# A two-block transformer on one core: the opening reordered across three engines, and the first output product opened with two tiles

## The reference, cut to what matters

```
def diff_attn_layer(x, norm_g, w_in, w_out, ...):
    h = rms_norm(x, norm_g)
    q, k, v, gate = jnp.split(h @ w_in, 4, axis=-1)
    q = partial_rope(q.reshape(B, L, 2 * A_HEADS, A_HEAD_DIM), cos, sin)
    k = partial_rope(k.reshape(B, L, 2 * A_HEADS, A_HEAD_DIM), cos, sin)
    ...
    o = diff_attention(q, k, v, lam, cid)            # 8 heads
    o = rms_norm(o, subln_g) * (1.0 - lambda_init)
    o = o.reshape(B, L, D_MODEL) * jax.nn.silu(gate)
    return x + o @ w_out
```

## Time and profile before

| | |
|---|---|
| time, median of 3 runs | 2648.57 us (2648.28 to 2649.2) |
| time of the profiled execution | 2649.55 us |
| its span, first to last instruction | 2647.7 us |
| mean granted TensorE clock | 0.989 |
| busy: TensorE, its weight load, VectorE, ScalarE, GpSimd | 98%, 92%, 37%, 46%, 72% |
| a load of half a weight tile (512 KB), issue to landing | 3.6 us (median) |

### The profile page before, as it was taken

One profiled execution on the slowest core, in us unless ns is written; L12 is line 12 of the kernel. 1 busy time (PEld: TensorE's weight loads), 2 busy tenths in 40 slices (PEclk: granted clock), 3 DMA queues, 4 the chain that ended last, 5 costly groups with the idle time before them and its releaser, 6 DMA issues.

```text
span 2647.7 us, 54457 instructions
## 1 busy us (share of the span) xinstructions
PE 2591.1 (98%) x22558; PEld 2442.5 (92%) x22558; DVE 978.4 (37%) x1361; ACT 1225.4 (46%) x1504; POOL 1902.3 (72%) x786
## 2 busy tenths in 40 slices
PE   7999999999999999999999999999999999999998
PEld 7899999999999999999898989999998898998986
DVE  5444444316666330314354544314371120120211
ACT  4344444555666654535353444345453343443443
POOL 5666677676666787757574757688698888888886
PEclk8999999999999999989999999999999999999999
DMA  5454455454444566545353535466566566666664
GB/s 187 138 156 143 144 147 156 129 175 138 135 145 142 151 184 213 151 120 163 115 160 109 161 112 160 128 191 209 158 177 188 178 189 203 186 187 190 185 189 151
DMA packets 119614, 426.51 MB, mean 161 GB/s; under 512 B 12784, under 2 KB 17008, under 8 KB 119152
## 3 DMA queue, kind: packets, MB, share of 16 engines
q1 hardware_dynamic: 114560, 416.55, 52.8%
q10 hardware_dynamic: 4848, 6.82, 0.8%
HBM read 419.12 MB, written 4.19 MB: 160 GB/s over the span
## 4 chain that ended last, share of the span: by engine, by line
PE 92%; DVE 4%; ACT 3%; issue 1%; DMA 0%; POOL 0%; SPq 0%; DVEq 0%; ACTq 0%; POOLq 0%
PE ps L315 15%; PE ps L218 15%; PE ps L220 15%; PE ps L227 15%; PE ps L241 5%; PE ps L249 5%; PE ps L243 5%; PE ps L1893 3%; PE ps L306 3%; PE ps L302 2%; PE ps L301 2%; PE ps L1183 2%; ACT wh L199 1%; PE ps L840 1%; PE ps L1785 1%; PE ps L1787 1%
## 5 line engine op out<-in xcount | busy, mean ns | idle before, releaser
L2886 POOL TENSOR_TENSOR wl<-raw,wh 128x1024 fp32r<-128x1024 f32 x782 | 1902.1, 2454 | 728.2 <-ACT wh L199 727.1
L199 ACT ACTIVATE wh<-raw 128x2048 fp32r<-128x2048 f32 x391 | 748.2, 1914 | 647.0 <-DMA raw<-weights 173.9
L218 PE MATMUL ps<-hh,wh 128*128 128x256 f32 (+1 forms) x3056 | 752.1, 285 | 3.5 <-DVE hl L351 2.3
L220 PE MATMUL ps<-hl,wh 128*128 128x256 f32 (+1 forms) x3056 | 749.0, 284 | 0.0
L218 PEld LDWEIGHTS ps<-hh,wh 128*128 128x128 f32 x3056 | 577.3, 189 | 8.6 <-issue 4.2
L220 PEld LDWEIGHTS ps<-hl,wh 128*128 128x128 f32 x3056 | 577.9, 189 | 0.1
L227 PE MATMUL ps<-hh,wl 128*128 128x256 f32 (+1 forms) x3056 | 398.2, 283 | 0.0
L227 PEld LDWEIGHTS ps<-hh,wl 128*128 128x128 f32 x3056 | 379.9, 188 | 0.3 <-POOL wl L2886 0.2
L315 PE MATMUL ps<-hh,wh 128*128 128x256 f32 x896 | 223.8, 290 | 0.0
L315 PE MATMUL ps<-hl,wh 128*128 128x256 f32 x896 | 215.6, 281 | 0.0
L241 PE MATMUL ps<-wh,gh 128*128 128x512 f32 x512 | 203.0, 397 | 0.0
(11 more groups left out here) (438 smaller groups left out, 3338.2 us busy)
## 6 DMA issues: line engine op xcount, KB each, us to landing
raw<-weights SPq DMA_DIRECT2D x782, 512.0 KB, 3.6
xT<-tokens SPq DMA_DIRECT2D x4, 544.0 KB, 7.1
spill<-xT ACTq DMA_DIRECT2D x1, 2048.0 KB, 13.4
xT<-spill ACTq DMA_DIRECT2D x1, 2048.0 KB, 10.3
out<-arena SPq DMA_DIRECT2D x4, 512.0 KB, 3.2
C<-consts SPq DMA_DIRECT2D x1, 2000.0 KB, 13.9
arena<-lora ACTq DMA_DIRECT2D x4, 384.0 KB, 3.2
arena<-rows ACTq DMA_DIRECT2D x1, 1024.0 KB, 6.6
```

The source lines that it names most:

```text
L199: nc.scalar.activation(wh[:, m % 2, :, :].rearrange("p a b -> p (a b)"), raw[:, 2 * (m % 2):2 * (m % 2) + 2, :, :].rearrange("p a b c -> p ...
L218: nc.tensor.matmul(acc[0:m, 0:n], wh[:, slot, kt, 0:m], rh[:, kt, 0:n], start=(kt == kts[0]), stop=False)
L220: nc.tensor.matmul(acc[0:m, 0:n], wh[:, slot, kt, 0:m], rl[:, kt, 0:n], start=False, stop=False)
L2886: nc.gpsimd.tensor_tensor(wl[:, s // 2, h, :], raw[:, s, :, :], wh[:, s // 2, h, :].bitcast(F32), ALU.subtract)\
```

## The change

1. ScalarE does a one-element Square on a constant before anything else. It makes `hh` of quarters 0 to 2 only, raising a step after every two blocks, rounds tile 0 behind quarter 0 and tile 1 behind quarter 2, and then squares all four quarters.
2. VectorE makes `hl` of quarters 0 and 1, then `hh` of quarter 3 (a new TENSOR_SCALAR), `hl` of 2 and 3, and then the four low halves of tiles 0 and 1, ahead of the additions of the squares. GpSimd's loop starts with tile 2 and waits for these four.
3. TensorE: in tiles 0 and 1 the order of parts changes ((0,3), (1,0), (1,1) now stand before (0,4)). `pe_sum` stands before part (2,3) instead of (2,4), `pe_all` and `lam_pe` before (3,0) instead of (3,2). `attn_a_sum` stands before part 3 instead of part 2.
4. `a_out`: tiles 0 and 1 are opened together by `opening_by_quarter`, without spins.

```diff
+        def opening_by_quarter(pe, phase_name, accs, rh, rl, n, split):
...
+            pe.wait_ge(hi_done, first_ + 1)
+            for k in range(2):
+                pe.wait_ge(split.V.sem, split.V.at(f"l{k}"))
+                high(0, range(4 * k, 4 * k + 4))
+            low(0, range(8))
+            pe.wait_ge(hi_done, first_ + 2)
+            high(1, range(8))
+            pe.wait_ge(split.V.sem, split.V.at("l2"))
+            high(0, range(8, 12))
+            low(0, range(8, 12))
+            high(1, range(8, 12))
+            low(1, range(12))
+            pe.wait_ge(split.V.sem, split.V.at("l3"))
+            high(0, range(12, KT))
+            low(0, range(12, KT)).then_inc(tile_done, 1)
+            high(1, range(12, KT))
+            low(1, range(12, KT)).then_inc(tile_done, 1)
...
         def start_act(act):
             A = SI["a"]
+            act.wait_ge(eps_set, 7)
+            nc.scalar.activation(st[:, 63:64], eps[:, 3:4], ACT.Square)
             act.wait_ge(p_in, 16)
-            for k in range(4):
+            for k in range(3):
                 act.wait_ge(x_in[k], 16)
                 for kt in range(4 * k, 4 * k + 4):
                     ins = nc.scalar.activation(hh[:, kt, :], xT[:, kt, :], ACT.Copy, scale=p("a", kt))
-                ins.then_inc(A.sem, A.step(f"h{k}"))
-                if k == 1:
+                    if kt % 2:
+                        ins.then_inc(A.sem, A.step(f"h{kt // 2}"))
+                if k == 0:
                     round_weights(act, "a", 0)
             round_weights(act, "a", 1)
-            start_squares(range(0, 2))
-
-        def start_squares(quarters):
-            A = SI["a"]
-            for k in quarters:
+            for k in range(4):
+                if k == 3:
+                    act.wait_ge(x_in[3], 16)
                 nc.scalar.activation(squares_a[:, k], xT[:, 4 * k:4 * k + 4, :], ACT.Square)\
                     .then_inc(A.sem, A.step(f"q{k}"))
...
+            rest(0)
+            rest(1)
+            dve.wait_ge(x_in[3], 16)
+            for kt in range(12, KT):
+                ins = nc.vector.tensor_scalar(hh[:, kt, :], xT[:, kt, :], p("a", kt), None, ALU.mult)
+            ins.then_inc(V.sem, V.step("hi"))
+            rest(2)
+            rest(3)
+            for s in range(4):
+                h = slice(8 * (s % 2), 8 * (s % 2) + 8)
+                dve.wait_ge(hi_done, s // 2 + 1)
+                nc.vector.tensor_tensor(wl[:, s // 2, h, :], raw[:, s, :, :], wh[:, s // 2, h, :].bitcast(F32),
+                                        ALU.subtract)\
+                    .then_inc(lo_done, 1)
...
-            for t, k in ((0, 0), (0, 1), (0, 2), (0, 4), (0, 3), (1, 0), (1, 1), (0, 5), (1, 2), (1, 3), (1, 4),
+            for t, k in ((0, 0), (0, 1), (0, 2), (0, 3), (1, 0), (1, 1), (0, 4), (0, 5), (1, 2), (1, 3), (1, 4),
                          (1, 5)):
...
-                            if (t, piece) == (2, 4):
+                            if (t, piece) == (2, 3):
                                 pe.wait_ge(cp_in, 16)
                                 factor_a.pe_sum(pe)
-                            if (t, piece) == (3, 2):
+                            if (t, piece) == (3, 0):
                                 factor_a.pe_all(pe)
                                 lam_pe(pe)
...
-                            if piece == 2:
+                            if piece == 3:
                                 attn_a_sum(pe, i - 1)
...
-                    if i == 0 and t == 0:
-                        start_squares(range(2, 4))
-                    elif i == 0:
+                    if i == 0 and t:
                         factor_a.act(act)
                         lam_act(act)
...
-            pool.wait_ge(SI["v"].sem, SI["v"].at("l3"))
-            with pool.Fori(0, N_TILES // 2) as i:
+            pool.wait_ge(lo_done, 4)
+            with pool.Fori(1, N_TILES // 2) as i:
```

More of the change, by code:

```diff
@@ L261, in opening @@
                     if kt % split.size == 0:
-                        if kt and phase_name == "a_out":
-                            spin(4, c("ident"), 6)
                         pe.wait_ge(split.V.sem, split.V.at(f"l{kt // split.size}"))
@@ L291, in opening_two, with high, low @@
                         ins.then_inc(tile_done, 1)
+        def opening_by_quarter(pe, phase_name, accs, rh, rl, n, split):
+            first_ = FIRST[phase_name]
+            def high(t, kts):
+                for kt in kts:
+                    nc.tensor.matmul(accs[t][:, 0:n], wh[:, (first_ + t) % 2, kt, :], rh[:, kt, 0:n], start=(kt == 0),
+                                     stop=False)
+                    nc.tensor.matmul(accs[t][:, 0:n], wh[:, (first_ + t) % 2, kt, :], rl[:, kt, 0:n], start=False,
+                                     stop=False)
+            def low(t, kts):
+                q = first_ + t
+                for kt in kts:
+                    if kt % 8 == 0:
+                        pe.wait_ge(lo_done, 2 * q + kt // 8 + 1)
+                    ins = nc.tensor.matmul(accs[t][:, 0:n], wl[:, q % 2, kt, :], rh[:, kt, 0:n], start=False,
+                                           stop=(kt == 15))
+                return ins
+            pe.wait_ge(hi_done, first_ + 1)
[15 more added lines that the diff above has]
+            low(1, range(12, KT)).then_inc(tile_done, 1)
         def part(pe, phase_name, t, k, acc, rh, rl, n):
@@ L593, in body @@
                             eng.wait_ge(self.V.sem, self.V.at(f"t{(t - 4) % 8}", i if t >= 4 else i - 1))
+                        if self.units == "a_out" and isinstance(i, int) and i == 0 and t < 2:
+                            if t:
+                                opening_by_quarter(eng, self.units, (ps[:, 0, :], ps[:, 1, :]), *self.rhs, self.n,
+                                                   self.split)
+                            continue
                         if first(i, t, self.split) and self.split.size == 4:
@@ L642, in dve_early @@
                 early.dve(eng, 15)
-        SI = phase("start", a="h0 h1 h2 h3 q0 q1 q2 q3",
-                   v=f"l0 l1 l2 l3 a0 a1 a2 f1 s{KT - 1} rs ck cm sk sm qs ns")
+        SI = phase("start", a="h0 h1 h2 h3 h4 h5 q0 q1 q2 q3",
+                   v=f"l0 l1 hi l2 l3 a0 a1 a2 f1 s{KT - 1} rs ck cm sk sm qs ns")
         squares_a = arena[:, ARENA - 16 * NT:ARENA].rearrange("p (k a n) -> p k a n", k=4, a=4)
@@ L717, in start_dve, with rest @@
             lam_products(dve)
-            for k in range(4):
-                dve.wait_ge(A.sem, A.at(f"h{k}"))
+            def rest(k):
                 for kt in range(4 * k, 4 * k + 4):
+                    if k < 3 and kt % 2 == 0:
+                        dve.wait_ge(A.sem, A.at(f"h{kt // 2}"))
+                    elif k == 3 and kt == 12:
+                        dve.wait_ge(V.sem, V.at("hi"))
                     ins = nc.vector.scalar_tensor_tensor(out=hl[:, kt, :], in0=xT[:, kt, :], scalar=p("a", kt),
```

## The result

| | before | after |
|---|---|---|
| median, runs side by side on one chip | 2648.81 us (4 runs) | 2622.23 us (4 runs, 2620.66 to 2625.09) |
| ratio | | 0.9901 [0.9884, 0.9918] |
| profiled execution | 2649.55 us | 2622.31 us |
| mean granted TensorE clock | 0.989 | 0.991 |

The changed kernel is 26.6 us (1.0%) faster. The forecast was 21.8 us, 2626.8; the result lies in its range, and where rival (a) had put it (2622.4). The two profiled executions lie 27.2 us apart.

What follows compares the result with a forecast made beforehand. TensorE, busy for 98% of the span, was taken as the bound. Gains of 13.2 + 1.2 + 3.7 + 3.7 = 21.8 us off the median of 2648.57 gave 2626.8 us, range 2620.5 to 2631.

Steps and rivals of the forecast that it cites:

- rival (a): Clock stays up at the scores, 4.4 us more gain, 2622.4; with a fast opening too, 2620.4; chance 0.28.
- Term 1: Opening up to tile 4 of the first product: tile 4 starts at 41.9 instead of 55.12, 13.2 us gained.
- the dummy Square: Opening on ScalarE: takes the 1.28 us table load ahead of the first tokens' arrival at 5.27 us.
- the estimate of 0.8 us: VectorE's four `hh` of quarter 3 by the tier formula; not adopted, 1.2 us forecast; worth under 0.3 us.
- Term 2: TensorE's wait for the turned queries ahead of the scores shrinks from 3.5 to 2.3 us: 1.2 us gained.
- The clock at the scores: Slow stretch of 8.75 us behind the scores' wait, costing about 4.4 us, was expected to stay.
- Term 3: Sums over `sqo` one part later: TensorE's seven waits, 3.7 us in total, vanish; 3.7 us gained.
- Term 4: Output product's opening, tiles 0 and 1 together: 3.7 us gained, with waits of 0.7, 1.3 and 0.8 us left.
- Nothing after 512 us is touched: Rest of the kernel behind the output product's opening: the gain arrives whole at the end, with no further change.
- (b): Part lost to late output product inputs and additions colliding with GpSimd: 2631.5 together; chance 0.17, including a short clock fall.
- (c): No change or nearly: a later bound, such as weight transfers, takes back the opening's slack; 2647; chance 0.03.
- (d): Slower: without spins the clock falls in the output product's opening and stays at 0.50; 2655; chance 0.02.

Runs made afterwards that it cites:

- the last experiment: Changed kernel plus five warm-up spins, fillers between the opening's first parts and nine spins ahead of the second attention's first tile: 2617.78 us, ratio 0.9893.
- the opposite experiment: Kernel before with one edit alone, the sum over the head's squares before part 3 instead of part 2: 2642.46 us, ratio 0.9985.

## Why the prediction was right, and where it was off

**Term 1, 13.2 us; measured 13.0.** Right, by its own steps: TensorE at 10.14 (10.0), clock back at 21.35 (21.5), additions done at 26.5 (26.9), tile 4 at 42.10 (41.9). Late squares take 11.0 us back (8.9 in the median), GpSimd's low halves 4.2 to 5.9; these are not shares of one sum. That the clock came back at 21.35 is in part luck: in the two repeats of the changed kernel it was back at 18.2 and 19.3, the first of them outside my bounds of 18.8 to 21.9, and tile 4 started at 40.45 and 41.13. One step was idle: the dummy Square is worth nothing measurable, because tile 0's weights land at 8.1. VectorE's four `hh` took 1.17 us, 0.29 each, as I took them from the row at 0.355. The trace doesn't bear out the estimate of 0.8 us that I made from the Trainium skill's tier table. The same page (VectorE: DVE Perf Modes, the section on the TRN2 errata) gives a larger measured fixed term, about 150 cycles an instruction, by which one would take 0.30 us, an estimate; with that the trace agrees, and I should have taken it.

**Term 2, 1.2 us; measured 3.7. This step was mis-sized,** in its cover. The forecast left a wait of 2.3 us; none was left. VectorE's chain of turned rows takes turns with GpSimd, and I let every instruction take its full turn. The addition at 44.35 fell into a pause between GpSimd's pairs of low halves (the next pair starts at 44.58) and took 0.71 us instead of 2.81. That is no chance of one execution, though the margin is thin: it took 0.71 us in both repeats too, 0.22 us ahead of the pair, and in every variant of the changed kernel but two, `pe_all` at (3, 2) and the last, where it starts 0.03 us behind the pair. Those 2.1 us, with the two parts of cover, brought the turned queries in at 53.6, ahead of 54.15. Where that addition meets GpSimd, the wait is back: 2.2 us in the last experiment, 3.5 with `pe_all` at its old place. The Trainium skill (GPSIMD Engine Reference, section 1, Specifications) says that the two engines share SBUF interfaces and contend when VectorE reads two SBUF inputs; this trace agrees, with 0.71 against 2.81 us for one shape.

**The clock at the scores, 0 in the sum; measured near 4.0.** This is rival (a), and it came true through the step above: with no wait at all, the stretch of 9.2 us behind 54.15 runs at 1.00. The 4.0 is the 9.5 us of the table less 5.5 for the sums; with the wait restored, 3.0 us of it went. That a wait of just over 2 us is followed by a fall, which kept it in my sum, is borne out: 2.2 us, then 7.3 us at 0.53. It is no law: the wait ahead of the second attention, 2.3 us before and 2.4 after, was followed by a fall in one of the two, and over all profiles here with a wait of 2.3 or 2.4 us at that place, in five of eleven. The Trainium skill (TensorE: Matmul & The Clock Gate, Part 1) calls the count of slow matmuls run-variable, since the monitor isn't tied to the kernel's start; the repeated profiles of the changed kernel agree, with 6.8 or 10.1 us of slow clock in the opening.

**Term 3, 3.7 us; measured 5.5.** Mechanism right, size off: I took the recorded wait of 0.53 us, where the gap that the sum opened in TensorE's stream was worth 0.79. That 5.5 comes from two profiles; the median of the opposite experiment gave 3.7, and its profile some 5.5.

**Term 4, 3.7 us; measured 3.8,** with waits of 0.45, 1.08 and 0.56 us (0.7, 1.3, 0.8). Tile 2's rounding was the next to be late, as forecast.

**"Nothing after 512 us is touched ... the shift should arrive whole."** It did not, quite: 29.9 us at 481 became 27.2 at the end. 1.7 us went up to the second attention's scores, nearly all in the fall of the clock behind its wait; 0.8 came back by the wide stretch in small steps that I can't explain; 1.6 went in that stretch, of which 3.3 us more were slow. Both falls change from one execution to the next (the first is absent in the two repeats), so this is the clock's scatter and no cost that I can tie to the change. In all, 13.0 + 3.7 + 9.5 + 3.8 - 2.7 = 27.3 us, against 27.2 between the spans. So the main sum was right in its path and low by the three terms above, and that the time fell on rival (a)'s 2622.4 is in part luck: the waits and gaps gave 2.5 and 1.8 us more than rival (a) had counted, and the scatter took 2.7 back. Rivals (b), (c) and (d) did not come: no addition met GpSimd in the opening, and no clock fell in the output product's.

## What to carry to other kernels

Where two engines take turns, what counts is whether a short chain of small instructions ends before the other engine's first large one starts; here moving two squares on a third engine was worth 9 us in the median and 11 at tile 4. Price a short wait by the distance between the starts of the matmuls around it rather than by the recorded wait, and add the slow stretch behind it where one is seen. Where an instruction in an alternation may fall into a pause, carry two values for it: one such case decided here between a wait of 2 us with a slow stretch behind it, and none, by a fraction of a microsecond in when it started.

## What the runs showed of the hardware that was not expected

- A VectorE addition of 32x544 takes 0.71 us in a pause of GpSimd and 2.8 to 2.9 us when it meets a 128x1024 subtraction there.
- The wide stretch of the mixer ran at 0.50 for 16.9 us before and 20.2 us after, with TensorE busy all through; over the experiments the slow part was between 6.9 and 20.6 us.
- The clock did not fall in either opening that was filled with small products (14.00 us at 1.00 in one). In the last experiment it then fell for 7 us at the scores, 40 us later, behind 2.2 us of idle time.
- A VectorE subtraction of 128x1024 took 1.23 us where it started 0.20 us ahead of a pair of GpSimd's subtractions, and 3.30 us where it started 0.13 us behind one.
